# Attention results written from PSUM as high and low parts into dead query tiles, memory score banks rotated, first weights and panel splits reordered

## What is computed

```python
def memory_cross_attention(h, m, w_q, w_kv, w_o):
    q = (h @ w_q).reshape(B, S, MEM_HEADS, MEM_HEAD_DIM)      # 4 heads of 256
    ...
    s = jnp.einsum('bshd,bmhd->bhsm', q, k).astype(jnp.float32) * (MEM_HEAD_DIM ** -0.5)
    p = jax.nn.softmax(s, axis=-1)
    o = jnp.einsum('bhsm,bmhd->bshd', p.astype(v.dtype), v).reshape(B, S, D_MODEL)
    return o @ w_o

def mla_mixer(h, w_q_a, g_q_latent, w_q_b, w_out, k_nope, k_rope, v, cos, sin):
    ...
    o = causal_mla_attention(q_nope, q_rope, k_nope, k_rope, v)   # 8 heads, values of 128
    return o.reshape(B_, S, B_HEADS * B_V) @ w_out
```

## Time and profile before

| | |
|---|---|
| runs | 2170.53, 2169.81, 2168.37 us; median 2169.81 us |
| profiled execution | 2171.98 us, of which the span of the instructions 2169.9 us |
| busy, share of the span | PE 97%, DVE 52%, POOL 45%, ACT 41% |
| chain that ended last | PE 60%, issue 21%, POOL 9%, DVE 5%, ACT 4%, DMA 1% |
| mean granted clock of PE | 0.987 of full speed (2.4 GHz) |

### The profile page before, as it was taken

One profiled execution on the slowest core, in us unless ns is written; L12 is line 12 of the kernel. 1 busy time (PEld: TensorE's weight loads), 2 busy tenths in 40 slices (PEclk: granted clock), 3 DMA queues, 4 the chain that ended last, 5 costly groups with the idle time before them and its releaser, 6 DMA issues.

```text
span 2169.9 us, 28079 instructions
## 1 busy us (share of the span) xinstructions
PE 2094.8 (97%) x9946; PEld 1702.7 (78%) x9946; DVE 1119.1 (52%) x1749; ACT 885.0 (41%) x1506; POOL 968.0 (45%) x489
## 2 busy tenths in 40 slices
PE   8999999989999999999999999999999999999997
PEld 5777787778888888787768888888777788888887
DVE  3534743334677776763473543434575435343435
ACT  4225874445222222434474422323465544323233
POOL 3436776343454444334123344444435623444443
PEclk9998999999999999999999999999999999999999
DMA  4440053204366664364102233333222012333332
GB/s 179 165 142 5 21 195 94 76 15 157 124 229 229 220 224 162 97 230 148 30 1 83 78 97 97 97 97 97 78 88 68 1 59 69 97 97 97 97 97 88
DMA packets 67925, 234.47 MB, mean 108 GB/s; under 512 B 7296, under 2 KB 10752, under 8 KB 67712
## 3 DMA queue, kind: packets, MB, share of 16 engines
q1 hardware_dynamic: 67840, 233.33, 33.1%
HBM read 231.20 MB, written 2.10 MB: 108 GB/s over the span
## 4 chain that ended last, share of the span: by engine, by line
PE 60%; issue 21%; POOL 9%; DVE 5%; ACT 4%; DMA 1%; POOLq 0%; SPq 0%; DVEq 0%; ACTq 0%
PE bank L892 18%; PE bank L893 17%; PE bank L894 17%; POOL WL L756 6%; PE bank L988 1%; PE bank L1111 1%; PE bank L1003 1%; DMA stage<-panels 1%; POOL sq L810 1%; PE bank L1176 0%; DVE acc L2286 0%; ACT WH L1581 0%; PE bank L1478 0%; POOL t L810 0%; PE bank L1210 0%
## 5 line engine op out<-in xcount | busy, mean ns | idle before, releaser
L756 POOL TENSOR_TENSOR WL<-stage,WH 128x1024 fp32r<-128x1024 f32 x264 | 657.2, 2491 | 943.3 <-ACT WH L1581 943.1
L1581 ACT ACTIVATE WH<-stage 128x1024 fp32r<-128x1024 f32 x264 | 279.8, 1060 | 828.5 <-PE bank L894 779.4
L892 PE MATMUL bank<-H,WH 128*128 128x512 f32 (+1 forms) x1324 | 510.2, 385 | 24.2 <-POOL WL L756 11.6
L893 PE MATMUL bank<-H,WH 128*128 128x512 f32 (+1 forms) x1324 | 507.8, 384 | 0.0
L894 PE MATMUL bank<-H,WL 128*128 128x512 f32 (+1 forms) x1324 | 507.3, 383 | 0.0
L892 PEld LDWEIGHTS bank<-H,WH 128*128 128x128 f32 x1324 | 250.6, 189 | 79.4 <-issue 21.5
L894 PEld LDWEIGHTS bank<-H,WL 128*128 128x128 f32 x1324 | 250.7, 189 | 48.8
L893 PEld LDWEIGHTS bank<-H,WH 128*128 128x128 f32 x1324 | 250.7, 189 | 48.0 <-issue 0.5
L2628 DVE TENSOR_TENSOR Y<-bank,Y 128x512 f32<-128x512 f32 x328 | 215.7, 684 | 94.8 <-PE bank L894 94.1
L892 PE MATMUL bank<-HID,WH 128*128 128x512 f32 (+1 forms) x688 | 264.3, 384 | 0.1
L893 PE MATMUL bank<-HID,WH 128*128 128x512 f32 (+1 forms) x688 | 264.2, 384 | 0.0
(11 more groups left out here) (435 smaller groups left out, 3365.9 us busy)
## 6 DMA issues: line engine op xcount, KB each, us to landing
stage<-panels SPq DMA_DIRECT2D x296, 512.0 KB, 3.7
ahead<-ada SPq DMA_DIRECT2D x96, 512.0 KB, 5.3
RAW<-panels SPq DMA_DIRECT2D x18, 512.0 KB, 4.4
apiece<-ada SPq DMA_DIRECT2D x16, 512.0 KB, 3.7
x<-xT SPq DMA_DIRECT2D x3, 1024.0 KB, 8.5
outT<-x SPq DMA_DIRECT2D x16, 128.0 KB, 1.7
x<-xT SPq DMA_DIRECT2D x2, 512.0 KB, 4.6
Y<-bias SPq DMA_DIRECT2D x1, 1024.0 KB, 6.0
```

Of the source, the lines that this page charges most:

```text
L756: pool.tensor_tensor(low_of(p, slot), stage[:, slot, :], high_of(p, slot).bitcast(F32), ALU.subtract).then_inc(s_split, 1)
L892: pe.matmul(out, wh, rh, start=start, stop=False)
L893: pe.matmul(out, wh, rl, start=False, stop=False)
L1581: act.activation(high_of(p, slot), stage[:, slot, :], ACT.Copy).then_inc(s_hisplit, 1)
```

## The change

There are four parts.

1. In mem and mla, ACT's `out(n)` writes a finished head from `O` to `QKH` as its high part (mla: tile `n`, which held the queries of head `n`, all scored by then; mem: tiles `2n` and `2n+1`, whose place held the memory's inputs and, from tile 4 on, keys that no score reads any more), and DVE's new `out_low(n)` writes `QKL` as `O` less `QKH`, at step `4n + 7` and for the last head after the loop. The copies to `Y`, the eight high copies and the eight low ones behind each attention go away. The projections read `QKH` and `QKL`. On PE `weigh` waits for the low parts in `s_h` (mem: of head `n - 1`; mla: of head `n - 2`) where it waited for ACT's copies. `WD` moves from 72 to 104.
2. Memory score banks are `[ST, AD, G[0], G[1]]`. PE waits for the low parts of query chunks 0 to 3 before the first two scores, for chunk 6 before the third, for chunk 7 before the fourth.
3. In all three attentions POOL does `scale` 0 to 2 before `low_v(0)`, and `scale(3)` before `low_v(1)`. ACT does `exp` 0 to 2 before `stage_v(0)`, and `exp(3)` before `stage_v(1)`.
4. POOL splits the panels `mem_k + 0` and `+ 1` after the self attention instead of before it.

```diff
+WEIGHED = {"mem": "o_mem", "mla": "o_b"}
...
-        WD = place(72, "WD", [P, 2, 2, D], F32R)
+        WD = place(104, "WD", [P, 2, 2, D], F32R)
...
-        score_bank = [G[0], G[1], ST, AD]
+        def score_bank(name, s):
+            return ([ST, AD, G[0], G[1]] if name == "mem" else [G[0], G[1], ST, AD])[s % 4]
+        def out_bank(name, n, c):
+            return O[c] if name == "mem" else O[n % 2]
+        def per_head(name):
+            return {"mem": 2, "mla": 1}[name]
...
             def attention(name):
                 steps = 4 * heads_of(name)
-                low_v(name, 0)
                 for s in range(3):
                     scale(name, s)
-                low_v(name, 1)
+                low_v(name, 0)
                 for s in range(steps):
                     if s + 3 < steps:
                         scale(name, s + 3)
+                    if s == 0:
+                        low_v(name, 1)
...
-            split_lows(4, PANEL0["mem_k"] + 2)
+            split_lows(4, PANEL0["mem_k"])
             attention("self")
+            split_lows(PANEL0["mem_k"], RING0)
...
-                        if n >= (1 if name == "mem" else 2):
-                            pe.wait_ge(sm["out"], n if name == "mem" else n - 1)
+                        if name == "self" and n >= 2:
+                            pe.wait_ge(sm["out"], n - 1)
+                        if name == "mem" and n:
+                            pe.wait_ge(s_h, before(MAKES, "o_mem") + 2 * n)
+                        if name == "mla" and n >= 2:
+                            pe.wait_ge(s_h, before(MAKES, "o_b") + n - 1)
...
                     for s in range(4):
+                        if name == "mem" and s >= 2:
+                            freed(pe, "mem_q", s + 5)
                         score(s)
...
-            freed(pe, "mem_q", 8)
+            freed(pe, "mem_q", 4)
...
+                    for c in range(per_head(name)):
+                        act.activation(QKH[:, per_head(name) * n + c, :], out_bank(name, n, c)[:, :], ACT.Copy)\
+                            .then_inc(s_hi, 1)
-                stage_v(0)
                 exp(0)
-                stage_v(1)
                 exp(1)
                 exp(2)
+                stage_v(0)
...
                     if s + 3 < steps:
                         exp(s + 3)
+                    if s == 0:
+                        stage_v(1)
...
-            act.wait_ge(att["mem"]["out"], 4)
-            high("o_mem", yc, hh)
...
+                def out_low(n):
+                    for c in range(per_head(name)):
+                        m = per_head(name) * n + c
+                        dve.wait_ge(s_hi, before(MAKES, WEIGHED[name]) + m + 1)
+                        dve.tensor_tensor(QKL[:, m, :], out_bank(name, n, c)[:, :], QKH[:, m, :].bitcast(F32), ALU.subtract)\
+                            .then_inc(s_h, 1)
...
+                    if name in WEIGHED and s >= 7 and s % 4 == 3:
+                        out_low((s - 7) // 4)
...
+                if name in WEIGHED:
+                    out_low(heads_of(name) - 1)
...
-            make_plain("o_mem", yc)
```

More of the change, by code:

```diff
@@ L925, in project @@
                 p0, first = PANEL0[name], 1
+                high, low = (QKH, QKL) if fresh in WEIGHED.values() else (H[:, :, 0, :], H[:, :, 1, :])
                 if name in JOINT:
@@ L1039, in last_chunks @@
                 p0 = PANEL0[proj]
+                high, low = (H[:, :, 0, :], H[:, :, 1, :]) if name == "a" else (QKH, QKL)
                 for half in range(2):
@@ L1100, in score_pair @@
                         pe.wait_ge(s_log, 2)
-                    first, second = scores(s // 8, s % 8 // 2, score_bank[s % 4], score_bank[s % 4 + 1])
+                    first, second = scores(s // 8, s % 8 // 2, score_bank(name, s), score_bank(name, s + 1))
                     first.then_inc(sm["scores"], 1)
@@ L1797, in self_norms, with attention @@
                     ring_panel(RING0 + (s - 61) // 2)
-            def attention(name, out_of, beside=None):
+            def attention(name, beside=None):
                 sm = att[name]
@@ L1834, in out @@
                     act.wait_ge(sm["pv"], weighed(name, n, 3))
-                    for dest, source in out_of(n):
-                        last = act.activation(dest, source, ACT.Copy)
-                    last.then_inc(sm["out"], 1)
-                stage_v(0)
+                    if name == "self":
+                        act.activation(Y[half_rows[n % 2], n // 2, :], O[n % 2][half_rows[n % 2], :], ACT.Copy)\
+                            .then_inc(sm["out"], 1)
+                        return
+                    for c in range(per_head(name)):
+                        act.activation(QKH[:, per_head(name) * n + c, :], out_bank(name, n, c)[:, :], ACT.Copy)\
+                            .then_inc(s_hi, 1)
                 exp(0)
-                stage_v(1)
                 exp(1)
                 exp(2)
+                stage_v(0)
                 for s in range(steps):
@@ L2004, in _ @@
             act.wait_ge(s_vev, 2 * NT + 1)
-            attention("self", lambda n: [(Y[half_rows[n % 2], n // 2, :], O[n % 2][half_rows[n % 2], :])], self_norms)
+            attention("self", self_norms)
             act.wait_ge(att["self"]["out"], 16)
@@ L2060, in _ @@
             evacuate_high("mem_q", lambda c: QKH[:, 8 + c, :], lambda c: 256 ** -0.5)
-            attention("mem", lambda n: [(Y[:, n * 2 + c, :], O[c][:, :]) for c in range(2)])
-            act.wait_ge(att["mem"]["out"], 4)
-            high("o_mem", yc, hh)
+            attention("mem")
             evacuate_halves("ca")
@@ L2255, in _ @@
             act.wait_ge(s_rql, 4)
-            attention("mla", lambda n: [(Y[:, n, :], O[n % 2][:, :])])
-            act.wait_ge(att["mla"]["out"], HEADS)
-            high("o_b", yc, hh)
+            attention("mla")
             evacuate_halves("b")
```

13 lines of the change are left out of this document (6 added, 7 removed).

## The result

| | before | changed |
|---|---|---|
| executions | 2170.53, 2169.81, 2168.37, 2172.56 us | 2157.66, 2156.90, 2155.31, 2157.27 us |
| median | 2170.17 us | 2157.09 us |
| ratio, 95% interval | | 0.9938 [0.992, 0.9955] |
| profiled execution, span | 2171.98, 2169.9 us | 2157.66, 2155.8 us |
| mean granted clock | 0.987 | 0.992 |

The forecast was 2161.0 us with a range from 2155.0 to 2167.5, so the change took off 13.1 us where the sum had 8.65. When the same kernel was timed again on chip 4 (first experiment), the gain of the medians came out at 6.8. Why one kernel gives both numbers is part of what follows.

The account below looks back on a forecast made before the run. PE, busy 97% of the span, was taken to bound the kernel through idle gaps and half clock. Terms -5.2, 0, -3.0, +4.8, +3.4, -5.85 and -2.8 summed to -8.65 us; forecast 2161.0 us, range 2155.0 to 2167.5.

Parts of the forecast that it names:

- start of self: Before self's first transpose: PE's 2.19 us gap goes, and 3.0 us of half clock behind it; -5.2 us.
- panel splits moved: POOL's two panel splits, now after self, end before PE wants them: 0 us, at most +4.8.
- start of mem: Before mem's first transpose: scores and DVE's first maximum start sooner, so the scaling moves earlier; -3.0 us.
- three added waits: Heads 1 to 3 of mem: PE waits for DVE's subtractions, 1.75, 1.75 and 1.3 us more; +4.8 us.
- clock behind them: Behind the gaps at heads 1 to 3 of mem: two of three slow stretches, 1.7 us each; +3.4 us.
- end of mem: Before `mem_o`: the 2.65 us gap goes, and both slow stretches behind the old gaps, 1.6 each; -5.85 us.
- mla, its end: Before `b_out`: the 2.17 us gap goes, and 0.6 of a slow stretch; inside mla 0; -2.8 us.
- only the gaps return: Slow stretches at self and `mem_o` stay, brought on by something besides the gaps: 2164.2 us; chance 0.13.
- rival of a free wait: Heads 1 to 3 of mem: subtractions find DVE free early, 4.8 and 3.4 fall away: 2152.9 us; chance 0.07.
- rival in which DVE bounds the loops: In mem and mla loops, ten subtractions push PE by 6.9 us, half clock adds 11: 2179 us; chance 0.04.
- 6.9 us that POOL might have lost beside them: Inside the loops: POOL would lose 0.69 us at each of ten subtractions if locked out; not expected, sum then -1.9.
- rival with a long stretch behind every wait: Heads 1 to 3 of mem: each wait slows the clock as long as at self, adding 5.9: 2167.0 us; chance 0.12.

Follow-up runs that it names:

- first experiment: The changed kernel timed again on chip 4 with no edit: 2160.71 us against 2167.51 for the kernel before, ratio 0.9958.
- the banks' experiment: Against the changed kernel, memory scores in banks G0, G1, ST, AD again and a wait for all eight query chunks: 2161.29 us, ratio 0.9961 to the kernel before.

## Why the prediction was right, and where it was not

The sum's terms, against the first pair of profiles (2171.98 to 2157.66, -14.3, of which the span 14.1):

| term | forecast | first pair of profiles | what all profiles say |
|---|---|---|---|
| start of self | -5.2 | -5.2 | holds when undone |
| panel splits moved | 0 | 0 | 0 |
| start of mem | -3.0 | -3.3 | 3.3 in the banks' experiment |
| three added waits | +4.8 | +4.6 | the same to 0.01 us each |
| clock behind them | +3.4 | +1.6 | about +2.4 |
| end of mem | -5.85 | -6.1 | -6 |
| mla, its end | -2.8 | -2.7 | -2.7 or -5.5 |
| self behind 245 us | not named | -2.0 | see below |
| before self, elsewhere | not named | -0.9 | differs by execution |

**Start of self.** The changed kernel is 0.82 us ahead where the value projection starts (145.51 before) and 6.04 ahead at self's next long gap (187.59 before), so 5.2 us were won between. The rival "only the gaps return" falls: full clock followed where the gap was gone, and with the undone orders the half clock returned together with the gap.

**Start of mem.** The mechanism held in all steps, but the whole gain was put down to the banks. Part 3 has a share: with value splits first the transpose waits 1.5 us for POOL. The prediction bounded POOL by its panel split alone and left out its value split of 1.27, which the banks by themselves would have had to wait for.

**The added waits.** 2.26, 2.96 and 3.25 us against the forecast 2.3, 3.0 and 3.3. Reading the queue of DVE in order, and adding 1.38 to the end of what stands ahead, was enough. The rival of a free wait falls as built; at heads 1 and 2 it comes true when the subtractions move one step. The rival in which DVE bounds the loops falls: mla takes 65.7 us with and without them. So do the 6.9 us that POOL might have lost beside them (with them the sum would have been -1.75, not the -1.9 of the prediction). Its scaling takes 0.93 us there, as the Trainium skill ("SBUF — State Buffer", section "Who interferes with whom") would have it for a DVE operation with one SBUF operand.

**Clock behind the waits.** I took two stretches of three. The eight profiles with the late subtractions show 2 behind head 1, 8 behind head 2 and 1 (of twice the length) behind head 3: 12 lengths of 3.4 us in 8 executions, 1.5 in each, some 2.4 us where 3.4 were forecast. The rival with a long stretch behind every wait came near in one profile, that with the value splits first. The Trainium skill's rule on bursts ("TensorE: Matmul & The Clock Gate", section "HAM oscillation — how this bites in real kernels") was a fair warning, and holds here only in part. Its example pays at every restart, with stops of about 3 to 5 us; the stops here were 2.3 to 3.3 us. The traces agree behind head 2, in 8 of 8, and not behind heads 1 and 3, in 3 of 16.

**End of mem, mla.** The two gaps went as forecast, and in the first pair of profiles so did the time (-2.7 at mla against -2.8). The one step that does not hold in all profiles is "only a part should go: -0.6, between 0 and -1.7": at `b_out` the half clock started before the old gap, in the last heads, and in eight of twelve profiles with direct writing it is gone altogether. Here the rows of the prediction began too late in time: the kernel before was at half clock from about 1737.8 to 1748.2, of which they show the end from 1744.60.

```profile
1738.70:1742.50 3.80, 3.78 (x12) 3.32 (x12) 0.00 (x0) 0.00 (x0) 0.00 (x0) 0.50 0.00 0
```

**What was not named.** Before, a gap of 1.68 us near 246 us was followed by 6.8 us at half clock.

```profile
247.93 0.41 PE L1111 MATMUL bank<-con,sq 128*128 128x128 f32 x2 [1.68 <-DVE PT L2567]
```

```profile
249.60:256.40 6.80, 6.80 (x36) 6.02 (x34) 4.53 (x16) 4.02 (x13) 5.60 (x4) 0.50 0.00 0
```

A stretch behind this gap is there in all four profiles with part 3 or 4 undone: 6.8 us long before and with value splits first, 3.4 long with both orders undone and with panel splits first. It is in none of the ten others, with the gap itself at 1.66 to 1.70. So it went with the reordering, 2.0 us in the first pair and 0.7 to 1.0 where it was short, though neither order touches that place. The gap at the start of self is not the link: with value splits first there was no such gap, and the stretch came. What links them was not found.

**The measurement.** The forecast of -8.65 lies between the two measured gains, -13.1 and -6.8, and close to the difference of means over 26 and 12 executions, -8.5. Four executions a side did not average the clock: the four of the changed kernel in the first result had 0.992 to 0.993, the twelve later ones 0.989 to 0.995. That the sum meets the -8.5 so closely is in part luck. All its slow stretches were read from one profile of the kernel before, with a clock of 0.987 and a cost of 28.2 us by (1 - clock) x span, where 26 executions average 23.2. Against that profile the changed kernel won 14.3, and the sum was short of it by 5.7, above all since it charged 1.8 too much for the clock behind the waits and had no term for the 2.0 behind 246 us and the 0.9 elsewhere. The gaps were forecast well one by one; how much half clock follows them differs by execution. (The sum gives 2161.2 against the median; the prediction wrote 2161.0.)

## What to carry to other kernels

When a new wait is put on the path, find what stands ahead of its producer in that engine's queue and where that engine idles: one step earlier on DVE, a change that earned nothing in mem as built earned 2.2 us of gaps there, and 5.8 with the half clock in the one profile taken. Cost a removed gap twice, once for itself and once for the half clock behind it, and read the second from several profiles, since the same gap may or may not be followed by it. When the edit is smaller than the spread of executions, compare stages of the traces between two fixed instructions, and medians only to confirm.

## What was not expected of the hardware

- A PE gap of one and the same length has different consequences. That of 2.96 us at head 2 of mem was followed by half clock in 8 of 8 profiles, that of 3.25 at head 3 in 1 of 8, that of 1.62 in self in 11 of 12. What decides it was not found.
- Constant matmuls that only fill such a gap kept the clock in both profiles that had them, against 1 of 12 without: 48 matmuls in the next 6.8 us instead of 24 in 6.6. They need a PSUM bank that nobody reads, which exists in self before its eighth step.
- One kernel's executions on one chip spread over 12 us (0.6%), and between its two ends the mean granted clock accounts for all of it: 2162.77 us at 0.992, 2174.98 us at 0.986, where (1 - clock) x span gives 17.3 and 30.4 us, 13.1 apart for 12.2 of time.
